# A transformer stack in fp32 on one core: the stretch up to the first MLP rewritten

## The reference, cut to what matters

```python
c_act = silu(c)                                    # 1024 values
mod = c_act @ ada_w[0] + ada_b[0]                  # ada_w[0] is 1024 x 6144, 24 MB
sh1, sc1, g1, sh2, sc2, g2 = split(mod, 6)
h = rmsnorm(x, norm_mix_g[0]) * (1 + sc1) + sh1
# pool mixer: 4 groups of 256 channels, windows 2, 4, 8, 16 along the sequence
pooled = (sum of h over the last w tokens) / min(t + 1, w) - h
x = x + g1 * (pooled @ pool_w[group]) * pool_scale
h = rmsnorm(x, norm_mlp_g[0]) * (1 + sc2) + sh2
x = x + g2 * (square(relu(h @ mlp_w1[0])) @ mlp_w2[0])
```

## Time and profile before

| | us |
|---|---|
| median of 3 runs (1975.31 to 1977.28) | 1975.54 |
| the profiled execution, whole | 1977.91 |
| its span, first to last instruction | 1976.5 |
| TensorE busy | 1820.3 (92%) |
| VectorE busy | 1051.8 (53%) |
| ScalarE busy | 647.4 (33%) |
| GpSimd busy | 82.6 (4%) |
| mean granted TensorE clock | 0.945 |

### The profile page before, as it was taken

The page is one execution under the profiler, slowest core; times in us unless marked ns, Lnnn a source line. Parts: engine busy times, 40 slices in busy tenths (PEclk is TensorE's granted clock), DMA queues, the critical chain, the costliest instruction groups (busy, mean ns, idle before and its releaser), DMA issues.

```text
span 1976.5 us, 21469 instructions
## 1 busy us (share of the span) xinstructions
PE 1820.3 (92%) x8828; PEld 1467.6 (74%) x8828; DVE 1051.8 (53%) x1336; ACT 647.4 (33%) x798; POOL 82.6 (4%) x87
## 2 busy tenths in 40 slices
PE   5659999999899899999999989967499999999997
PEld 2238888888678688888886868846388888888885
DVE  4874675467545543244345574453656542566523
ACT  2123312321333342134334423433344431244412
POOL 2400010001000000000000101100000000000000
PEclk8669999999899899999998989988699999999997
DMA  9713375257222223232322420002032332323221
GB/s 356 282 64 107 119 245 169 90 188 239 80 88 84 85 86 106 86 107 86 106 91 69 97 69 4 4 1 85 22 107 94 98 95 98 102 90 106 87 85 43
DMA packets 124000, 208.55 MB, mean 106 GB/s; under 512 B 13965, under 2 KB 48421, under 8 KB 123904
## 3 DMA queue, kind: packets, MB, share of 16 engines
q1 hardware_dynamic: 115424, 174.94, 27.3%
q0 software_dynamic: 7808, 29.43, 4.5%
q10 hardware_dynamic: 672, 2.82, 0.4%
HBM read 204.01 MB, written 4.73 MB: 106 GB/s over the span
## 4 chain that ended last, share of the span: by engine, by line
PE 87%; DVE 8%; ACT 1%; DMA 1%; issue 1%; SPq 1%; DVEq 0%; ACTq 0%
PE bank L531 74%; DVE ada_acc L1672 2%; DMA ada_ring<-in_ada_w 1%; PE bank L898 1%; PE bank L547 1%; PE bank L881 1%; PE bank L861 1%; SPq L476 1%; PE bank L542 1%; DVE gT L2015 1%; PE bank L618 1%; DVE outer L2013 0%; PE bank L943 0%; PE bank L673 0%; PE bank L922 0%
## 5 line engine op out<-in xcount | busy, mean ns | idle before, releaser
L1597 DVE TENSOR_TENSOR w_lo<-raw,w_hi 128x2048 fp32r<-128x2048 f32 x138 | 316.2, 2292 | 503.4 <-ACT w_hi L1160 503.4
L1160 ACT ACTIVATE w_hi<-raw 128x2048 fp32r<-128x2048 f32 x138 | 263.8, 1912 | 606.7 <-PE bank L531 584.7
L531 PE MATMUL bank<-u_hi,w_hi 128*128 128x512 f32 x768 | 300.5, 391 | 0.8 <-DVE conv L2271 0.8
L531 PE MATMUL bank<-u_hi,w_lo 128*128 128x512 f32 x768 | 299.0, 389 | 0.0
L531 PE MATMUL bank<-u_lo,w_hi 128*128 128x512 f32 x768 | 298.8, 389 | 0.0
L531 PE MATMUL bank<-h_hi,w_hi 128*128 128x512 f32 x736 | 291.8, 396 | 5.1 <-DVE h_lo L1644 5.1
L531 PE MATMUL bank<-h_lo,w_hi 128*128 128x512 f32 x736 | 288.6, 392 | 0.0
L531 PE MATMUL bank<-h_hi,w_lo 128*128 128x512 f32 x736 | 288.5, 392 | 0.0
L531 PE MATMUL bank<-f_hi,w_hi 128*128 128x512 f32 x512 | 200.4, 391 | 2.4 <-DVE f_lo L1647 2.4
L531 PE MATMUL bank<-f_lo,w_hi 128*128 128x512 f32 x512 | 199.9, 390 | 0.0
L531 PE MATMUL bank<-f_hi,w_lo 128*128 128x512 f32 x512 | 199.7, 390 | 0.0
(11 more groups left out here) (351 smaller groups left out, 2038.6 us busy)
## 6 DMA issues: line engine op xcount, KB each, us to landing
raw<-in_mlp_w SPq DMA_DIRECT2D x128, 512.0 KB, 4.5
raw<-in_w_ffn_up SPq DMA_DIRECT2D x64, 512.0 KB, 4.5
ada_ring<-in_ada_w POOLq DMA_DIRECT2D x24, 1024.0 KB, 5.9
ada_ring<-in_ada_w SPq DMA_DIRECT2D x9, 2048.0 KB, 13.2
raw<-in_w_ffn_down SPq DMA_DIRECT2D x32, 512.0 KB, 4.4
raw<-in_w_in SPq DMA_DIRECT2D x20, 512.0 KB, 4.4
raw<-in_sgu_w_in SPq DMA_DIRECT2D x16, 512.0 KB, 4.9
x_rows<-in_ada_w SPq DMA_DIRECT2D x3, 2048.0 KB, 11.8
```

What stands on the lines that cost most here:

```text
L531: mm = te.matmul(bank[:, n], a, b, start=first and k == 0 and j == 0, stop=last and k == 3 and j == 2)
L1160: se.activation(m.ring(s)[0], m.raw[:, slot], ACT.Copy).then_inc(sem("hi_made"), 1)
L1597: ve.tensor_tensor(lo, m.raw[:, slot], hi.bitcast(F32), ALU.subtract).then_inc(sem("lo_made"), 1)
```

## The change

The first stretch:

- The loads of the modulation come in the order 2, 3, 0, 1, 4, 5, 6, 8, 7, 9, 10, 11 (scale of the mixer first). Each of the first ten is shared: VectorE sums columns 0 to 255 in eight steps of 128x256 (`ada_half`), TensorE does columns 256 to 511 with the loaded weights as stationary operand and one column of `c_act` moving: 2 x 8 products for each load (`ada_products`), then two sums over partitions of VectorE's half (`ada_sums`). TensorE's results stand directly in the wanted layout. Loads 10 and 11 stay whole on VectorE, beside groups 0 and 1 of the MLP (`late`), with eight sums on TensorE behind group 2. SyncE issues two loads behind slab 0 and two behind slab 1.
- The input arrives in four DMAs. ScalarE squares its token rows with an accumulated sum, VectorE scales the rows (`xn`), and TensorE makes the sliding means, less the value itself, as products with band matrices read from memory (`windows`: 8 x 4 products with 144 or 128 moving columns). GpSimd computes nothing any more. The gain and the shift are put on afterwards (`pooled(k)`).
- The squares before the first MLP are no longer added by VectorE: TensorE sums all eight tiles (`norm_mean_of_all`: 32 products with one moving column).
- VectorE's order before the first slab: inverse, half of load 7, gain, tiles 0 to 3 of `h`, `w_lo` of slab 0; then the halves of loads 8 and 9, tiles 4 to 7, `w_lo` of slab 1. Slab 0 runs with k outermost; the products of load 8 stand between its third and fourth k, those of load 9 behind it.

Later in the program:

- Norms `MIX1`, `MLP1`, `POST`, `LAST`: additions of squares are placed behind the single tiles, the eighth square is summed apart on TensorE (four more products).
- Norm `FFN`: `norm_mean_of_all`, no additions on VectorE.
- The norm at the end of the projection `w_out` squares from PSUM ahead of the copy.
- In the projection of the second block, ScalarE's copy of the spread (`first_copied`) goes ahead of the `w_hi` of a slab.

The diff, cut to its core:

```diff
+ADA_ORDER = (2, 3, 0, 1, 4, 5, 6, 8, 7, 9, 10, 11)
+ADA_SLOT = (0, 1, 2, 3, 0, 1, 2, 3, 0, 2, 1, 3)
+LAST_APART = (NORM_MIX1, NORM_MLP1, NORM_POST, NORM_LAST)
+SUMMED_ON_PE = (NORM_MLP0, NORM_FFN)
...
 (sync_program)
+    def modulation(i):
+        g, slot = ADA_ORDER[i], ADA_SLOT[i]
+        if slot in ADA_SLOT[:i]:
+            before = max(n for n in range(i) if ADA_SLOT[n] == slot)
+            sy.wait_ge(sem("ada_columns"), before + 1)
+        sy.dma_start(m.ada_ring[:, slot], ...)
+    for i in range(8):
+        modulation(i)
...
 (tensor_program)
+    def norm_mean_of_all(norm, squares):
+        for k in range(DT):
+            te.wait_ge(sem("squared"), 8 * norm + k + 1)
+            for j in range(4):
+                mm = te.matmul(bank[:, 4, j:j + 1], squares[:, k, P * j:P * j + P], m.mean_ones[:, 0:1], ...)
...
+    def windows(k):
+        g = k // 2
...
+        for j in range(4):
+            n = P + 16 if j < 3 else P
+            mm = te.matmul(bank[:, k % 4, P * j:P * j + n], m.xn[:, j, P * k:P * k + P], m.bands[:, min(j, 1), g, 0:n], ...)
...
+    def ada_products(i):
+        g, slot = ADA_ORDER[i], ADA_SLOT[i]
+        if i >= 2:
+            te.wait_ge(sem("mod_made"), i - 1)
...
+        te.wait_ge(sem(f"ada_in{slot}"), 16 * ADA_SLOT[:i + 1].count(slot))
+        for c in (2, 3):
+            for k in range(8):
+                te.matmul(bank[:, 6 + i % 2, 4 * g + c:4 * g + c + 1], m.ada_ring[:, slot, k, P * c:P * c + P],
+                          m.c_act[:, k:k + 1], start=k == 0, stop=k == 7)
+    def ada_sums(i):
+        te.wait_ge(sem("ada_step"), 8 * i + 8)
+        for c in range(2):
+            mm = te.matmul(..., m.ada_ring[:, slot, 0, P * c:P * c + P], ones[:, 0:1], ...)
+    for i in range(4):
+        ada_products(i)
+        ada_sums(i)
+    for i in range(4, 6):
+        for o in range(3 * (i - 4), 3 * (i - 4) + 3):
+            mix_pool(o)
+        ada_products(i)
+        ada_sums(i)
+    mix_pool(6)
+    mix_pool(7)
+    ada_products(6)
+    ada_sums(6)
-    norm_mean(NORM_MLP0, m.sq_b[:, 3])
+    norm_mean_of_all(NORM_MLP0, m.pooled)
...
 (vector_program)
+    for i in range(4):
+        ada_half(i)
+        if i:
+            mod(i - 1)
...
+    def first_norm():
+        inverse_and_diagonal(NORM_MLP0)
+        ada_half(7)
+        half_gain(7, 0)
...
+        normalise_lo(NORM_MLP0, ..., range(4))
+        split_to(0)
+        ada_half(8)
+        ada_half(9)
+        mod(8)
+        half_gain(9, 4)
+        normalise_lo(NORM_MLP0, ..., range(4, 8))
+        split_to(1)
+    def late(g):
+        if g < 2:
+            i = 10 + g
+            ada(i, 512, m.ada1_acc[:, 2 * g:2 * g + 2].rearrange("p a n -> p (a n)"))
...
 (scalar_program)
+    for j in range(4):
+        se.wait_ge(sem(f"x_in{j}"), 16)
+        se.activation(m.xn[:, j], m.x_rows[:, j], ACT.Square, accum_out=m.x_ms[:, j:j + 1])
...
-    split_to(first + 3)
     se.wait_ge(sem("spread"), NORM_FINAL + 1)
     se.activation(m.first_rstd, m.rstd_bank, ACT.Copy).then_inc(sem("first_copied"), 1)
+    split_to(first + 3)
```

More of the change, by code:

```diff
@@ L509, in emptied, with slab @@
         te.wait_ge(sem(f"{engine}_emptied"), count)
-    def slab(s, group, hi, lo, first, last, before_k=None, before_n=None, weights_stationary=True, k_outer=False, after_n=None):
+    def slab(s, group, hi, lo, first, last, before_k=None, before_n=None, weights_stationary=True, k_outer=False, after_n=None, after_k=None):
         w_hi, w_lo = m.ring(s)
@@ L599, in tensor_program @@
+    for k in range(DT):
+        windows(k)
     te.wait_ge(sem("rel_in"), 48)
     te.wait_ge(sem("rel_masked"), MILESTONE["rel_masked"])
[L601 to L610, removed]
@@ new lines, in mix_pool @@
+    def mix_pool(o):
+        g, n = o // 2, o % 2
+        if o >= 6:
+            te.wait_ge(sem("x_mixed"), o - 5)
+        if o == 4:
+            te.wait_ge(sem("table_made"), MILESTONE["table_made"])
+        if o == 0:
+            te.wait_ge(sem("pool_w_in"), 16)
+        if n == 0:
+            te.wait_ge(sem("pooled_made"), 2 * g + 2)
+        if o < 4:
+            te.wait_ge(sem("windows_copied"), o + 5)
+        for k in range(2):
+            mm = te.matmul(bank[:, o % 6], m.pool_w[:, g, k, P * n:P * n + P], m.pooled[:, 2 * g + k], start=k == 0, stop=k == 1)
+        mm.then_inc(sem("pool_full"), 1)
@@ L1530, in scalar_program @@
             full(s + 1, group, n)
+            if g:
+                square(NORM_POST, 4 + n, bank[:, n], squares)
             se.activation(m.mixed[:, 4 * g + n], bank[:, n], ACT.Copy).then_inc(sem("act_emptied"), 1)
-    for o in range(4, 8):
-        emptied(GROUPS["w_out"] + 1, o - 4)
-        square(NORM_POST, o, m.mixed[:, o], squares)
     root(NORM_POST)
@@ new lines, in vector_program, with ada @@
+    n = own.on(ve.reciprocal(m.x_ms[:, :], m.x_ms[:, :]))
+    ve.wait_ge(own.sem, n)
+    for j in range(4):
+        ve.tensor_scalar(m.xn[:, j], m.x_rows[:, j], m.x_ms[:, j:j + 1], None, ALU.mult).then_inc(sem("x_normed"), 1)
+    def ada(i, columns, acc):
+        slot = ADA_SLOT[i]
+        if i == 0:
+            ve.wait_ge(sem("silu_made"), MILESTONE["silu_made"])
+        ve.wait_ge(sem(f"ada_in{slot}"), 16 * ADA_SLOT[:i + 1].count(slot))
+        ve.tensor_scalar(acc, m.ada_ring[:, slot, 0, 0:columns], m.c_act[:, 0:1], None, ALU.mult).then_inc(sem("ada_step"), 1)
@@ L1772, in mlp @@
                     ve.tensor_tensor(u_lo[:, 4 * g + n], sq[:, n], u_hi[:, 4 * g + n].bitcast(F32), ALU.subtract).then_inc(sem("u_lo_made"), 1)
+                if layer == 0 and half == 0:
+                    late(g)
             for g in range(2):
@@ L1793, in mlp @@
                         gained_lo(o)
-        for o in range(4, 8):
-            add_square(next_norm, o, sq)
-            if layer:
+                    elif half and g and n:
+                        add_square(next_norm, o - 1, sq)
+        if layer:
+            for o in range(4, 8):
+                add_square(next_norm, o, sq)
                 add_second_square(o)
@@ L1824, in ada1_add @@
             ada1["added"] = u + 1
[L1826 to L1829 removed]
+    mlp(0, NORM_MLP0, NORM_MIX1, None, None, m.u_hi, m.u_lo, m.sq_b, ada1_add)
     ve.wait_ge(sem("ada1_summed"), ADA1_LOADS)
@@ L2241, in vector_program @@
                     add_square(NORM_POST, o, squares)
[L2242 removed]
+    for o in range(4, 7):
         add_square(NORM_POST, o, squares)
```

476 lines of the change are left out of this document (222 added, 254 removed).

## The result

| | before | after |
|---|---|---|
| median of the runs, us | 1975.54 (1975.31 to 1977.28) | 1984.47 (1982.58 to 1987.10) |
| ratio to before, 95% interval | | 1.0039 (1.0023 to 1.0055) |
| profiled execution, us | 1977.91 (span 1976.5) | 1984.47 (span 1983.1) |

The kernel became slower by 0.4%. The forecast was 1980.2, slower, with 1955 to 1992 as its range. The range held, and the direction. The change is +8.9 us by the medians and +6.6 by the spans of the profiled executions, for a forecast of +4.7; three of its terms were off, and their errors offset each other in part.

A forecast was written before the change was run, and what follows sets the result against it. TensorE, busy 92% of the span, was taken as the bound, with its start and pauses changeable. First stretch +19.6 and later norms -14.9 gave +4.7 on the profiled 1977.91, 1982.6; less 2.4 to the median, 1980.2 us; range 1955 to 1992.

The forecast's parts named there:

- The clock: Shared modulation loads: long one-column runs fall to half clock after about the first load, 8.0 us a load instead of 4.4.
- records of 0.22 us: Sign for the forecast: `ada_products` records at 0.22 us each, against 0.12 us at full clock.
- The rival of a full clock: One-column products in the modulation hold the full clock once the windows raised it: -35 us, 1940; chance 0.15.
- The first stretch, step by step,: From the start through slab 2 of the first MLP: slab 2 at 180.2 for 163.7, +16.5 us; +19.6 with late loads and sums.
- my own bound of 176: Lower bound for the start of slab 2 in the first MLP, forecast at 180.2 us (bounds 176 and 185).
- before 170: Sign of being wrong: slab 2 of the first MLP begins before 170 us, which only the clock can do.
- The late loads: Behind slab 2's start: VectorE's 512-column `late` loads delay `w_lo`, +0.4 to 0.8 us twice, taken as +1.2.
- The later norms: Norms behind the first MLP: fewer additions shorten TensorE's waits before the means, -14.9 us in sum (bounds -9 and -21).
- the 9 us: Sign of being wrong: the later norms give less than 9 us.
- At FFN: Norm before the last FFN: 32 sums at half clock, 16.4 us to the mean's end instead of 17.5, put at -1.5.
- At FINAL: Copy ahead of `w_hi`: wait 2.96 to 1.1 us, eight records 7.16 to perhaps 3.6; -1.9 to -6.5, taken as -3.5.
- the slow rival: First stretch: x or first load late (1986), or clock never rises before slab 0 (some 2015); chance 0.18 together.

The follow-up runs named there:

- experiments 1 and 2: Kernel after with TensorE's modulation products streaming 128 columns (1963.16 us); then also the sums of squares before the first MLP and at FFN (1953.42 us).
- Experiment 3: Kernel after with the outer loop over input tiles (k outermost) in slab 0 only, no longer in slab 1: 1978.34 us, ratio 1.0003.
- experiment 4: Kernel before with only the edits to the norms behind the first MLP, its first stretch untouched: 1966.41 us, ratio 0.9939.
- experiment 6: Kernel after with wide modulation products and sums of squares, k outermost in slab 0 only, earlier weight splits, and key-norm products streaming 32 columns: 1932.63 us, ratio 0.9771.
- experiments 4 and 7: The second of the two: kernel after with VectorE taking 384 of a load's 512 columns, TensorE 128, nothing wide: 1968.81 us, ratio 0.9951.

## Why the prediction was right, and where not

**The clock.** Right, and decisive: half clock in long runs of one-column products, full only for the first load. I named records of 0.22 us as the sign, and 6.97 / 32 is 0.218. The rival of a full clock (1940, chance 0.15) did not happen by itself; experiments 1 and 2 brought it about with the wide operand, and end at 1953.

**The first stretch, step by step,** forecast and measured:

| end of | forecast | measured |
|---|---|---|
| windows | 28 | 26.2 |
| loads 0 to 3 | 57.5 | 53.7 |
| load 4, 5, 6 | 70, 82.5, 95.7 | 65.3, 76.7, 89.2 |
| mean | 109.9 | 102.8 |
| load 7 | 122 | 113.7 |
| slab 0 starts | 131.4 | 122.8 |
| slab 0 and load 8 | 150.5 | 141.3 |
| slab 1 starts | 167.5 | 156.8 |
| slab 2 starts | 180.2 | 169.8 |

Nearly every step was forecast a little too long and none by much: windows 1.8, loads 0 to 3 another 2.0 (7.68 us apart, not 8.0; the second still a little faster), the three behind them 2.7, the mean 0.6, load 7 1.2, the tiles ahead of slab 0 0.3, slab 0 with load 8 0.6, slab 1 with load 9 1.2. The errors had one sign, so they added up. Slab 2 came at +6.1 instead of +16.5, below my own bound of 176. It also came before 170, which I had named as a sign of being wrong, "which only the clock can do". By that sign the schedule was wrong, and the reason given with it too: the clock was as forecast (0.53 from 34 to 60 us), and many small terms did it.

**The late loads.** This step failed: "3.0 + 6.0 + 2.3 for `w_lo` is 11.3 against the 10.9 of slab 2, so +0.4 to 0.8 twice". I took the last `u_lo` at 3.0 us behind slab 2's start from the kernel before. In the kernel after slab 1 also runs with the outer loop over input tiles, so it ends 7.1 us behind it (176.9 for 169.8); and slab 3 then started cold. 4.34 of waiting and 1.8 of restart and cold start make +6.1, not +0.4 to 0.8. Experiment 3 shows this cause. The second late load, at slab 4, cost 0.4 as forecast, the late sums 2.0, and the first stretch is +14.5 for a forecast of +19.6.

**The later norms.** Near one by one, MIX1 apart: -2.7, -1.5, -4.1, -4.9, -1.5 and -2.3 for -1.6, -1.4, -3.5, -4.7, -1.5 and -2.2, -17.0 in all for -14.9. What I left out is 8.7 us of lower clock between them (1.6 + 0.4 + 3.9 + 2.0 + 0.8); the sum put this at nothing. Net, the norms gave 8.3 us in the kernel after and 7.4 in experiment 4, where -14.9 was to be the whole change. Both are under the 9 us that I had named as a sign of being wrong, though what the norms gave at their own places is well above it.

Three small sums of the prediction don't come out as written. At FFN, 17.5 less 16.4 is 1.1, not 1.5 (1.5 was measured). At FINAL, 1.9 and 3.6 make 5.5, not the bound of 6.5. In the slow rival, three loads stand behind group products, not the six that its 18 us need.

**The sum.** +14.5 - 17.0 + 8.7 = +6.2 at TensorE's last products; 0.5 more come behind them, for a difference of the spans of 6.6 and a forecast of +4.7. That it came out so near is luck in good part: the first stretch was forecast 5.1 too slow, the norms gave 2.1 more than forecast, and the clock's losses of 8.7 stood at nothing.

## What to carry to other kernels

Price a long run of products with one moving column at the clock that it will leave behind, not at the one that it finds. Where such runs are on the path, pad the moving operand: 128 columns cost 0.2 us more than one in 16 products at the full clock, and saved 3.2 at half. A saved wait is not yet a saved time: 17.0 us at the norms were 8.3 at the end. Where an outer loop's order is changed to start sooner, ask when its outputs complete, since the engine behind it plans by that; and let weights be split ahead of the tiles that come last.

## What the hardware showed that I had not expected

- Busy all the time and still near half: 26.00 of 26.00 us at a granted clock of 0.56 with one-column products, 24.03 of 26.00 at 0.93 with 128 columns, the same weights loaded.
- The same instructions lose the clock in one kernel and keep it in another: 14.4 or 12.8 us at the gated unit, 19.6 or 16.4 at the key norms, 195.7 to 200.2 in the recurrence (table in experiment 6). All kernels but the one before have the norms' edits; the kernel after and experiments 4 and 7 lost at all three places, experiment 3 only 0.2 us, in the recurrence. Why the level falls at one place and not another was not settled.
- Twelve runs of experiment 3 lie between 1974.63 and 1984.17 us, seventeen of the kernel before between 1976.09 and 1981.75. Whether the schedule is the cause was not tested.
